# Scan: differences by products of 18 rows, and the diagonal with its inputs as stationary operand

## The chip, the cores and the metric

The kernel runs on one core of a Trainium2 chip. The metric is the device time in microseconds of one execution; the time of the kernel before is a median of three runs. Below, TensorE is the matrix engine (PE in the rows, PEld its weight loads), VectorE is DVE, ScalarE is ACT, GpSimd is POOL, and SyncE (SP, its queue SPq) issues the transfers.

## The reference

The program is one layer of a hybrid block over 16 meta tokens and 2048 frames of width 1024: an input projection, a stick-breaking attention, a Mamba-2 scan (SSD), an output projection. The change touches the scan alone, whose chunks the kernel makes 128 steps long:

```python
xdt = x * dt[..., None]
a_cum = jnp.cumsum(dt * a.reshape(G, R), axis=2)
seg = a_cum[:, :, :, None] - a_cum[:, :, None]
decay_ls = jnp.exp(jnp.where(causal, seg, -jnp.inf))
cb = jnp.einsum("bclgn,bcsgn->bclsg", cm, bm)
y_diag = jnp.einsum("bclsg,bclsgr,bcsgrp->bclgrp", cb, decay_ls, xdt)
decay_to_end = jnp.exp(a_cum[:, :, -1:] - a_cum)
states = jnp.einsum("bclgn,bclgr,bclgrp->bcgrpn", bm, decay_to_end, xdt)
chunk_decay = jnp.exp(a_cum[:, :, -1])
def step(h, inp):
    st, dec = inp
    return h * dec[..., None, None] + st, h
y_off = jnp.einsum("bclgn,bcgrpn,bclgr->bclgrp", cm, h_start, jnp.exp(a_cum))
y = y_diag + y_off + x * d_skip.astype(f32).reshape(G, R)[:, :, None]
```

There are 16 heads of 64 columns in two groups of 8 (G, R = 2, 8), and a state of 128 rows. `seg` is the difference of two running sums; only its exponential for later minus earlier steps is used.

## The kernel before, in words

The program runs four stages one behind the other: front (the input projection), the scan's setup (`scan_start`) and the scan (`scan_stage`), attention, output. A stage ends for all engines together, and each stage loads what the next one needs first where it can.

The scan has 16 chunks of 128 steps (`NT`), two groups of 8 heads each, so 32 units (s, g, i): s is the parity of the chunk, g the group, i the pair of chunks. The buffers of the inputs, `xc` (x, B and C of one chunk) and `zt` (its gate), are there twice, one for each s. `pipeline` writes out the order on each engine: at step n it calls a list of parts, each with how many units ahead of n it works. On TensorE the order in a step is front(n+1), turn(n-1), multiply(n). front makes, for g = 0, the transposes of B and C·B (`pbc`) and the running sums (`pc`), then for every unit the transposes of x (`px`) and the differences (`pseg`); turn transposes the sum of unit n-1 for its store (into `pyd`); multiply makes the product with the old state (`pyo`), the new state's part (`pst`) and the diagonal part (`pyd`). On GpSimd the order is spread_steps(n+2), skip(n+1), gate(n-1). All products are float32.

`before(s, g, i)` gives the unit ahead of one, so that a bank is not overwritten before its reader is done. SyncE stores and loads in one written order, and a wait in it holds back all that stands behind:

```python
store(s, 0, i)
if more:
    sp.wait_ge(off_done[s][1], i + 1 + START)
    sp.wait_ge(xd_ready[s][1], i + 1 + START)
    scan.load_xc(sp, s, i + 1)
store(s, 1, i)
if more:
    scan.load_zt(sp, s, i + 1)
```

So the load of the inputs of chunk c+1 is issued behind the store of group 0 of chunk c-1, which waits for `gate` of that unit on GpSimd; and front of the first unit of chunk c+1 waits on TensorE for the load (`xc_loaded`). Of the 16 loads of `xc` two are made by the setup and 14 by this loop.

Of the kernel before, what the change touches and what calls it, by code (L numbers as in the profile page):

```python
# [18 lines left out]
ALU = mybir.AluOpType  # L19
ACT = mybir.ActivationFunctionType  # L20
# [18 lines left out]
HPG = HEADS // GROUPS  # L39
CONV = 4  # L40
# [1149 lines left out]
class ScanEarly(Early):  # L1190


    def __init__(self, nc, ctx, scratch, d_cols):
# [6 lines left out]
        self.zt = [self.sbuf(f"s_zt{s}", [P, KB, P]) for s in range(2)]  # L1200
        self.d_loaded, self.filled, self.made = self.sem("d_loaded"), self.sem("s_filled"), self.sem("s_made")
# [32 lines left out]
def scan_start(nc, scratch, dt_tok, state, scan, attention):  # L1234

    with ExitStack() as ctx:
# [10 lines left out]
        ps = m.psum("s0_ps", [P, GROUPS, W])  # L1247
        loaded, made, ready = m.sem("s0_loaded"), m.sem("s0_made"), m.sem("s0_ready")
# [13 lines left out]
        def _(pool):  # L1262
            nc.gpsimd.memset(ident[:, :], 0.0).then_inc(made, 1)
# [6 lines left out]
            scan.constants(pool)  # L1270
# [3 lines left out]
        def _(pe):  # L1274
            pe.wait_ge(ready, START + 2)
# [13 lines left out]
        def _(act):  # L1289
            act.wait_ge(turned, START + 1)  # L1290
# [4 lines left out]
        def _(dve):  # L1295
            dve.wait_ge(turned, START + 1)
# [12 lines left out]
def scan_stage(nc, scratch, dt_tok, state, scan, attention):  # L1309
# [5 lines left out]
    with ExitStack() as ctx:  # L1315
# [6 lines left out]
        expo = [m.sbuf(f"s_expo{s}", [P, 3, HEADS]) for s in range(2)]  # L1322
        cbm = [m.sbuf(f"s_cbm{s}", [P, GROUPS, P]) for s in range(2)]
        ua = [m.sbuf(f"s_ua{g}", [P, HPG, P]) for g in range(GROUPS)]
# [5 lines left out]
        ysum = [m.sbuf(f"s_ysum{g}", [P, W]) for g in range(GROUPS)]  # L1330
# [5 lines left out]
        pc = m.psum("s_pc", [P, 3, HEADS])  # L1336
# [22 lines left out]

        def dt_of(i, s, which, g):  # L1360
# [3 lines left out]
            return dt_tok[:, bass.ds(i * 2 + (1 + s), 1), which, g * HPG:(g + 1) * HPG].rearrange("p o h -> p (o h)")  # L1364

# [21 lines left out]
        def _(sp):  # L1387
# [24 lines left out]
        def _(pool):  # L1412
# [22 lines left out]
            pipeline(pool, (2, spread_steps), (1, skip), (-1, gate))  # L1435

        @block.tensor
        def _(pe):
            pe.wait_ge(made, START + 4)

            def front(s, g, i):
                if g == 0:
# [9 lines left out]
                    pe.wait_ge(expo_ready[1 - s], i + s + START)  # L1452
                    for n, lhs in enumerate((upper, later, ones)):
                        rhs = (dt_tok[:, 1 + 2 * i + s, 1, :] if isinstance(i, int) else
                               dt_tok[:, bass.ds(i * 2 + (1 + s), 1), 1, :].rearrange("p o h -> p (o h)"))
# [846 lines left out]
```

## Time and profile before

| what | before |
|---|---|
| median of 3 runs | 2749.34 us (2748.38 to 2751.9) |
| profiled execution | 2747.44 us, of which 2745.6 us are the span of the trace |
| mean granted clock of TensorE | 0.973 |
| PE busy | 2606.7 us (95%) |
| PEld busy | 1834.4 us (67%) |
| DVE busy | 1770.6 us (64%) |
| ACT busy | 1311.5 us (48%) |
| POOL busy | 1586.4 us (58%) |
| the scan's first instructions | 1155.00 us |
| the attention's first instructions | 1394.77 us |

Shares are of the whole span. Positions in the trace are in us from its start, and the granted clock is a share of 2.4 GHz: 1.00 is that level, 0.50 is 1.2 GHz.

### The profile page before, as it was taken

The numbers are of one execution on the slowest core, as the hardware profiler recorded it, in microseconds if no ns is written. First come the engines' busy times: TensorE is split into PE (matmuls) and PEld (weight loads), VectorE is DVE, ScalarE is ACT, GpSimd is POOL, SyncE is SP. The second block draws the span as 40 slices with busy tenths as digits, with TensorE's granted clock in tenths as the row PEclk, the third lists the DMA queues.
The fourth block names the chain that finished last, engine by engine and source line by source line (L and its number), as shares of the span: only waits on it lengthen the run. The fifth ranks groups of instructions, "written<-read, shape, count | busy, mean of one in ns | idle before, by whom it ended". The sixth has DMA issues, their size and how long they took to land. (4 is left out here: it accounts for less than half of the span.)

```text
span 2745.6 us, 41086 instructions
## 1 busy us (share of the span) xinstructions
PE 2606.7 (95%) x14122; PEld 1834.4 (67%) x14122; DVE 1770.6 (64%) x2152; ACT 1311.5 (48%) x2072; POOL 1586.4 (58%) x1222
## 2 busy tenths in 40 slices
PE   5999999989999999799989999999999999599998
PEld 3788777767888888566645555555555555388887
DVE  5532565644214554299969888898888889555554
ACT  4433333434333333211158777787778777322221
POOL 5876666688777777478746565665666666000000
PEclk7999999999999999899979999999999999799999
DMA  2543323323333323244541212303122111333231
GB/s 104 154 157 111 124 86 132 116 89 129 128 123 138 123 99 132 70 115 131 148 135 55 71 49 61 93 24 93 55 62 78 40 40 58 123 119 107 76 113 40
DMA packets 202405, 267.95 MB, mean 98 GB/s; under 512 B 12833, under 2 KB 136033, under 8 KB 195569
## 3 DMA queue, kind: packets, MB, share of 16 engines
q1 hardware_dynamic: 202224, 265.64, 30.4%
q8 instruction: 102, 1.67, 0.3%
q14 instruction: 79, 0.64, 0.1%
HBM read 168.84 MB, written 96.76 MB: 97 GB/s over the span
## 5 line engine op out<-in xcount | busy, mean ns | idle before, releaser
L1969 POOL TENSOR_TENSOR a_w<-a_beta,a_rest 128x1024 f32<-128x1024 f32 (+2 forms) x320 | 560.3, 1751 | 354.0 <-DVE a_rest L1926 207.3
L763 POOL TENSOR_TENSOR f_l_lo<-f_wst,f_l_hi 128x512 fp32r<-128x512 f32 x312 | 405.0, 1301 | 269.1 <-ACT f_l_hi L631 268.8
L1926 DVE TENSOR_TENSOR_SCAN a_rest<-a_keep,a_rest,a_ones 128x513 f32<-128x513 f32 x384 | 470.0, 1262 | 10.8 <-ACT a_keep L1896 10.8
L1846 PE MATMUL a_turn<-a_ident,a_w 128*128 128x128 f32 (+1 forms) x2432 | 342.9, 279 | 7.3 <-DVE a_wt L1880 6.1
L1861 PE MATMUL a_o<-a_wt,a_v 128*64 128x512 f32 (+3 forms) x1408 | 339.4, 560 | 8.9 <-DVE a_out L1936 8.9
L499 PE MATMUL f_xz<-f_t_hi,f_l_hi 128*128 128x512 f32 x832 | 330.2, 397 | 6.9 <-issue 4.4
L499 PE MATMUL f_xz<-f_t_hi,f_l_lo 128*128 128x512 f32 x832 | 326.3, 392 | 0.0
L499 PE MATMUL f_xz<-f_t_lo,f_l_hi 128*128 128x512 f32 x832 | 326.0, 392 | 0.0
L1880 ACT COPY a_wt<-a_turn 128x512 f32<-128x512 f32 (+3 forms) x440 | 225.1, 528 | 207.0 <-PE a_turn L1846 205.5
L1846 PEld LDWEIGHTS a_turn<-a_ident,a_w 128*128 128x128 f32 (+1 forms) x2432 | 256.7, 140 | 91.5 <-issue 65.8
L1896 ACT ACTIVATE a_keep<-a_z 128x1024 f32<-128x1024 f32 (+4 forms) x352 | 300.1, 852 | 4.6 <-PE a_z L1829 4.5
L1896 ACT ACTIVATE a_beta<-a_z 128x1024 f32<-128x1024 f32 (+4 forms) x352 | 300.2, 853 | 0.0
L631 ACT ACTIVATE f_l_hi<-f_wst 128x512 fp32r<-128x512 f32 x312 | 195.9, 628 | 201.7 <-PE f_y L499 105.3
L499 PE MATMUL f_y<-f_t_hi,f_l_hi 128*128 128x512 f32 x624 | 248.6, 398 | 10.0 <-DVE f_work L1125 6.5
L499 PE MATMUL f_y<-f_t_lo,f_l_hi 128*128 128x512 f32 x624 | 244.7, 392 | 0.0
L499 PE MATMUL f_y<-f_t_hi,f_l_lo 128*128 128x512 f32 x624 | 244.3, 392 | 0.0
L1926 DVE TENSOR_TENSOR_SCAN a_rest<-a_keep,a_ones 128x144 f32<-128x144 f32 (+3 forms) x256 | 206.9, 837 | 44.5 <-ACT a_keep L1896 44.4
L1819 PEld LDWEIGHTS a_z<-a_k_high,a_q_high 64*128 64x128 f32 x704 | 66.6, 186 | 248.6 <-issue 219.2
L2143 PE MATMUL o_acc<-o_w_hi,o_g_hi 128*128 128x512 f32 x512 | 202.8, 396 | 20.8 <-DVE o_w_lo L2197 17.7
L1880 DVE COPY a_wt<-a_turn 128x512 f32<-128x512 f32 (+3 forms) x264 | 158.5, 600 | 71.9 <-PE a_turn L1846 71.2
L2143 PE MATMUL o_acc<-o_w_hi,o_g_lo 128*128 128x512 f32 x512 | 200.7, 392 | 0.0
L2143 PE MATMUL o_acc<-o_w_lo,o_g_hi 128*128 128x512 f32 x512 | 200.5, 392 | 0.0
(242 smaller groups left out, 4472.7 us busy)
## 6 DMA issues: line engine op xcount, KB each, us to landing
f_wst<-in_w_pairs SPq DMA_DIRECT2D x52, 1024.0 KB, 5.5
scratch_gate<-f_out SPq DMA_DIRECT2D x64, 256.0 KB, 2.2
o_g<-scratch_mixed SPq DMA_DIRECT2D x32, 512.0 KB, 5.5
s_xc<-scratch_xbc SPq DMA_DIRECT2D x16, 768.0 KB, 5.3
scratch_xbc<-f_out SPq DMA_DIRECT2D x36, 256.0 KB, 2.1
scratch_q_hi<-f_out SPq DMA_DIRECT2D x32, 256.0 KB, 3.5
scratch_q_lo<-f_out SPq DMA_DIRECT2D x32, 256.0 KB, 3.6
scratch_v<-f_out SPq DMA_DIRECT2D x32, 256.0 KB, 2.3
```

The costliest lines, as they stand in the source:

```text
L499: last = nc.tensor.matmul(BANKS[i][:, :], lhs[:, k, :], rhs[:, k, :], start=(i < 3 and k == 0 and lhs is hi and rhs is t_hi[i]), stop=(k = ...
L631: nc.scalar.activation(l_hi[m % RING][:, :, :], left_source(n, i), ACT.Copy).then_inc(left_hi, 1)
L763: return nc.gpsimd.tensor_tensor(out, a, b, op).then_inc(done, 1)
L1819: mm = nc.tensor.matmul(z[n % 2][:, h, 0:tn], q_part[ch % 2][rows, qb * P:(qb + 1) * P], k_part[slot][rows, t0:t0 + tn], start=(i == 0), s ...
L1846: mm = nc.tensor.transpose(turn[h][0:rows, qi * P:(qi + 1) * P], tile[:, h, x:x + rows], ident[:, :])
L1861: mm = nc.tensor.matmul(o[h * HEAD:(h + 1) * HEAD, first_q:W], v[pair % 2][0:rows, b, h * HEAD:(h + 1) * HEAD], wt[m % ATS][0:rows, h, fir ...
L1880: copy(wt[m % ATS][0:rows, h, first_q:W], turn[h][0:rows, first_q:W]).then_inc(done, 1)
L1896: nc.scalar.activation(tile[side(n) % KEEPS][:, :, lo:lo + tn], z[n % 2][:, :, 0:tn], ACT.Sigmoid, scale=scale).then_inc(done, 1)
L1926: mm = nc.vector.tensor_tensor_scan(rest[r % RS][:, h, tn - 1::-1], top, ones[:, 0:1].to_broadcast([P, tn]), start, ALU.mult, ALU.min)
L1969: nc.gpsimd.tensor_tensor(w[r % AS][:, :, 0:tn], beta[r % KEEPS][:, :, 0:tn], rest[r % RS][:, :, 1:tn + 1], ALU.mult).then_inc(w_ready, 1)
L2143: mm = nc.tensor.matmul(acc[n][q][:, :], lhs[s][:, k, :], rhs[:, k, n * W:(n + 1) * W], start=(k == q * KB and lhs is g_hi and rhs is w_hi ...
```

## The change

- The differences. Before, GpSimd spread the steps of 8 heads over a triangle (`ua`, 128x1024 values a unit), and TensorE multiplied it by a triangle of ones over 128 rows in float32. Now the setup makes the running sums of all chunks by step, splits each in a high and a low part (float32r), and writes them to memory (`scratch["cum"]`); each unit loads them back as two operands of 18 rows: `lag` (16 rows with the sums of 8 heads in two parts, two rows of ones) and `rise` (16 constant rows of -1 that select a head, two rows with the sums). The product of both is the difference, in float32r. ScalarE then makes two passes in place of one: Relu with scale -1, and Exp with scale -1.
- The running sums. The three small products and their exponential (`pc`, `expo`) leave the loop; the setup makes them for all chunks (`sums`).
- The diagonal. Before, the weights `mt` were the stationary operand and 64 columns of `xdt` moved, 8 products a unit. Now 64 columns of `xdt` are the stationary operand and 128 columns of `mt` move, 8 products, even heads into partitions 0 to 63 and odd ones into 64 to 127; the result is already transposed.
- The offset. `yo` is no longer added on VectorE (`ysum` is gone) and then transposed; it is multiplied by the identity in a float32 product that adds to `pyd`.
- Two operations move from VectorE to GpSimd: `xde` (to_end) and the decay of the state (fade), in front of skip and gate.
- SyncE issues 6 small loads more for each chunk, and the setup 4 small stores and 12 small loads.

The diff, cut:

```diff
+    def load_spans(self, sp, s, g, i):
+        steps = self.scratch["cum"][:, bass.ds(i * 2 + s, 1), g * HPG:(g + 1) * HPG, :]
+        sp.dma_start(self.rise[s][g][SPANS - 2:SPANS, :, :].bitcast(F32),
+                     steps.rearrange("q o h l -> q (o h) l")).then_inc(self.rise_loaded[s][g], 16)
+        for q in range(2):
+            sp.dma_start(self.lag[s][g][q * HPG:(q + 1) * HPG, :].bitcast(F32),
+                         steps[q, :, :, :].rearrange("o h l -> (o h) l")).then_inc(self.rise_loaded[s][g], 16)
...
+            scan.constants(pool)
+            nc.gpsimd.memset(own[:, :, :], 0.0).then_inc(own_step, 1)
+            for q in range(2):
+                pool.wait_ge(own_step, START + q + 1)
+                nc.gpsimd.affine_select(out=own[:, :, :], in_=own[:, :, :], compare_op=ALU.not_equal, fill=-1.0,
+                                        base=-q * HPG, pattern=[[-1, HPG], [0, P]], channel_multiplier=1).then_inc(own_step, 1)
...
+                    if more:
+                        for g in range(GROUPS):
+                            sp.wait_ge(seg_ready[s][g], i + 1 + START)
+                            scan.load_spans(sp, s, g, i + 1)
                     store(s, 0, i)
...
-            def spread_steps(s, g, i):
-
-                pool.wait_ge(seg_ready[1 - s][g], i + s + START)
-                nc.gpsimd.tensor_tensor(ua[g][:, :, :], upper[:, :].unsqueeze(1).to_broadcast([P, HPG, P]),
-                                        over_heads(dt_of(i, s, 1, g), P), ALU.mult).then_inc(ua_ready[s][g], 1)
+            def to_end(s, g, i):
+
+                hs = slice(g * HPG, (g + 1) * HPG)
+                pool.wait_ge(xdt_ready[s][g], i + 1 + START)
+                pool.wait_ge(st_done[1 - s][g], i + s + START)
+                nc.gpsimd.tensor_tensor(heads(xde[g]), heads(xdt[g]), over_heads(sums_of(i, s, 1, hs), HEAD),
+                                        ALU.mult).then_inc(xde_ready[s][g], 1)
+
+            def fade(s, g, i):
+
+                hs = slice(g * HPG, (g + 1) * HPG)
+                pool.wait_ge(off_done[s][g], i + 1 + START)
+                own = state[:, g, :].rearrange("p (h c) -> p h c", h=HPG)
+                nc.gpsimd.tensor_tensor(own, own, over_heads(sums_of(i, s, 2, hs), HEAD), ALU.mult).then_inc(decayed[s][g], 1)
...
-            pipeline(pool, (2, spread_steps), (1, skip), (-1, gate))
+            pipeline(pool, (1, to_end), (0, fade), (1, skip), (-1, gate))
...
-                    last = nc.tensor.matmul(pseg[:, hs, :], later[:, :], ua[g][:, hs, :], start=True, stop=True)
+                    last = nc.tensor.matmul(pseg[:, hs, :], scan.lag[s][g][:, :], scan.rise[s][g][:, hs, :], start=True, stop=True)
...
-                    last = nc.tensor.transpose(pyd[:, b * P:(b + 1) * P], ysum[g][:, b * P:(b + 1) * P], ident[:, :])
+                    last = nc.tensor.matmul(pyd[:, b * P:(b + 1) * P], yo[g][:, b * P:(b + 1) * P], ident[:, :],
+                                            start=False, stop=True, skip_group_check=True)
...
-                    last = nc.tensor.matmul(pyd[:, h * HEAD:(h + 1) * HEAD], mt[g][:, h, :],
-                                            xdt[g][:, h * HEAD:(h + 1) * HEAD], start=True, stop=True)
+                    rows, cols = slice(h % 2 * HEAD, (h % 2 + 1) * HEAD), slice(h // 2 * P, (h // 2 + 1) * P)
+                    last = nc.tensor.matmul(pyd[rows, cols], xdt[g][:, h * HEAD:(h + 1) * HEAD], mt[g][:, h, :],
+                                            start=(h < 2), stop=False, skip_group_check=True)
...
-                nc.scalar.activation(decay[g][:, :, :], pseg[:, :, :], ACT.Exp).then_inc(decay_ready[s][g], 1)
+                nc.scalar.activation(decay[g][:, :, :], pseg[:, :, :], ACT.Relu, scale=-1.0).then_inc(span_ready[s][g], 1)
+                act.wait_ge(span_ready[s][g], i + 1 + START)
+                nc.scalar.activation(decay[g][:, :, :], decay[g][:, :, :], ACT.Exp, scale=-1.0).then_inc(decay_ready[s][g], 1)
...
-                own = state[:, g, :].rearrange("p (h c) -> p h c", h=HPG)
-                nc.vector.tensor_tensor(own, own, over_heads(expo[s][:, 2, hs], HEAD), ALU.mult).then_inc(decayed[s][g], 1)
                 dve.wait_ge(decayed[s][g], i + 1 + START)
...
-            pipeline(dve, (1, inputs), (-1, add_skip), (0, states), (1, weights), (0, sum_y))
+            pipeline(dve, (1, inputs), (-1, add_skip), (0, states), (1, weights))
```

On TensorE, one unit with g = 1 in the loop, before (`pseg` the differences, the first `pyd` row the transposes of turn, the last one the diagonal):

```order
L1461 MATMUL s_px<-s_ident,s_xc 128x128 x4
L1467 MATMUL s_pseg<-s_ua,s_later 128x512 x2
L1473 MATMUL s_pyd<-s_ident,s_ysum 128x128 x4
L1480 MATMUL s_pyo<-state,s_xc 128x512
L1485 MATMUL s_pst<-s_xde,s_b 128x512
L1489 MATMUL s_pyd<-s_xdt,s_mt 128x64 x8
```

and now:

```order
L1540 MATMUL s_px<-s_ident,s_xc 128x128 x4
L1546 MATMUL s_pseg<-s_rise,s_lag 128x512 x2
L1552 MATMUL s_pyd<-s_ident,s_yo 128x128 x4
L1560 MATMUL s_pyo<-state,s_xc 128x512
L1565 MATMUL s_pst<-s_xde,s_b 128x512
L1570 MATMUL s_pyd<-s_mt,s_xdt 64x128 x8
```

The order is the same; the turn is a product of `yo` and stands ahead of `pyo` as before, and the diagonal has 128 moving columns in place of 64.

On GpSimd, two units ahead of the loop, before, with buffer numbers, which are the group's (`ua` is spread_steps, `xd` skip, `gated` gate):

```order
L1419 TENSOR_TENSOR s_ua1<-s_upper,dt_tok 128x1024
L1425 TENSOR_TENSOR s_xd0<-s_xc1,s_d_col 128x512
L1432 TENSOR_TENSOR s_gated0<-s_yt0,s_zt0 128x512
L1419 TENSOR_TENSOR s_ua0<-s_upper,dt_tok 128x1024
L1425 TENSOR_TENSOR s_xd1<-s_xc1,s_d_col 128x512
L1432 TENSOR_TENSOR s_gated1<-s_yt1,s_zt0 128x512
```

and now (`xde` is to_end, `state` fade):

```order
L1497 TENSOR_TENSOR s_xde0<-s_xdt0,s_sums 128x512
L1505 TENSOR_TENSOR state<-state,s_sums 128x512
L1510 TENSOR_TENSOR s_xd0<-s_xc1,s_d_col 128x512
L1517 TENSOR_TENSOR s_gated0<-s_yt0,s_zt0 128x512
L1497 TENSOR_TENSOR s_xde1<-s_xdt1,s_sums 128x512
L1505 TENSOR_TENSOR state<-state,s_sums 128x512
L1510 TENSOR_TENSOR s_xd1<-s_xc1,s_d_col 128x512
L1517 TENSOR_TENSOR s_gated1<-s_yt1,s_zt0 128x512
```

The gate of a unit has moved behind fade, an operation that waits for `pyo` of the unit after it.


## Rows read from the trace of the kernel before

**Rows 1.** Stretch of the scan: length, PE, PEld, DVE, ACT, POOL busy, PEclk, DMA share, GB/s

```profile
1210.00:1240.00 30.00, 29.72 (x171) 20.88 (x170) 29.05 (x37) 5.89 (x10) 24.40 (x14) 1.00 0.47 124
```

**Rows 2.** Timeline of the scan; start us, us, engine, line, operation, tiles

```profile
1251.95 1.58 DVE L1540 TENSOR_TENSOR s_mt<-s_decay,s_cbm 128x1024 f32<-128x1024 f32 x1
...
1252.02 0.44 PE L1447 MATMUL s_pbc<-s_ident,s_xc 128*128 128x128 f32 x2 [0.25 <-DMA s_xc<-scratch_xbc]
...
1252.40 2.88 POOL L1419 TENSOR_TENSOR s_ua<-s_upper,dt_tok 128x1024 f32<-128x1024 f32 x1
...
1252.74 0.29 PE L1456 MATMUL s_pc<-dt_tok,s_upper 128*128 x2
...
1253.33 0.63 PE L1461 MATMUL s_px<-s_ident,s_xc 128*128 128x128 f32 x4
...
1253.80 1.88 PE L1467 MATMUL s_pseg<-s_ua,s_later 128*128 128x512 f32 x4
...
1255.52 0.60 PE L1473 MATMUL s_pyd<-s_ident,s_ysum 128*128 128x128 f32 x4
...
1255.95 1.02 PE L1480 MATMUL s_pyo<-state,s_xc 128*128 128x512 f32 x2
...
1257.67 1.90 PE L1489 MATMUL s_pyd<-s_xdt,s_mt 128*128 128x64 f32 x16
...
1259.40 0.61 PE L1461 MATMUL s_px<-s_ident,s_xc 128*128 128x128 f32 x4
...
1259.89 0.39 SPq L1390 DMA_DIRECT2D scratch_mixed<-s_gated  x1
...
1260.54 0.38 SPq L1205 DMA_DIRECT2D s_xc<-scratch_xbc  x1
...
1265.80 0.44 PE L1447 MATMUL s_pbc<-s_ident,s_xc 128*128 128x128 f32 x2
```

**Rows 3.** DMA issues of the page; times, KB each, median us to landing

```profile
s_xc<-scratch_xbc SPq DMA_DIRECT2D x16, 768.0 KB, 5.3
```

**Rows 4.** Timeline, TensorE alone, attention

```profile
1906.18 1.08 PE L1861 MATMUL a_o<-a_wt,a_v 128*64 128x512 f32 x4
```

**Rows 5.** Timeline of the last products ahead of the scan

```profile
1120.35 0.39 PE L499 MATMUL f_y<-f_t_hi,f_l_hi 128*128 128x512 f32 x1
...
1120.58 0.39 PE L499 MATMUL f_y<-f_t_lo,f_l_hi 128*128 128x512 f32 x1
```

**Rows 6.** Instructions that touch four tiles of the scan; ns min/median/max

```profile
L1419 POOL TENSOR_TENSOR s_ua<-s_upper,dt_tok x32: 1894/2874/2882, 1155.0 to 1363.6; 128x1024 f32<-128x1024 f32 x32
...
L1432 POOL TENSOR_TENSOR s_gated<-s_yt,s_zt x32: 1261/1718/1727, 1174.8 to 1388.2; 128x512 f32<-128x512 f32 x32
...
L1425 POOL TENSOR_TENSOR s_xd<-s_xc,s_d_col x32: 1038/1039/2019, 1158.7 to 1374.4; 128x512 f32<-128x512 f32 x32
...
L1540 DVE TENSOR_TENSOR s_mt<-s_decay,s_cbm x32: 1220/1573/1966, 1163.2 to 1376.6; 128x1024 f32<-128x1024 f32 x32
```

**Rows 7.** Costliest groups, ScalarE; xcount, busy us, mean ns, idle before

```profile
L1507 ACT ACTIVATE s_decay<-s_pseg 128x1024 f32<-128x1024 f32 x32 | 32.8, 1025 | 112.0 <-PE s_pseg L1467 112.0
```

**Rows 8.** Timeline, end of the scan

```profile
1378.87 1.11 PE L1473 MATMUL s_pyd<-s_ident,s_ysum 128*128 128x128 f32 x4 [2.29 <-DVE s_ysum L1560]
```

**Rows 9.** Timeline, TensorE alone, a gap in the attention

```profile
2129.10 1.97 PE L1861 MATMUL a_o<-a_wt,a_v 128*64 128x512 f32 x4 [1.11 <-DVE a_out L1936]
```

**Rows 10.** Timeline of the setup in front of the scan

```profile
1139.69 0.28 POOL L1226 TENSOR_SCALAR_AFFINE_SELECT s_upper<-s_upper 128x128 f32<-128x128 f32 x1
...
1140.45 4.50 SPq L1209 DMA_DIRECT2D s_zt<-scratch_gate  x2
...
1140.93 1.86 PE L1278 MATMUL s_px<-s_ident,s_xc 128*16 128x128 f32 x8 [8.18 <-DMA s_xc<-scratch_xbc]
...
1149.81 1.23 DVE L1306 COPY state<-s_ps 128x1024 f32<-128x1024 f32 x1 [3.93 <-PE s_ps L1285]
1155.00 3.75 POOL L1419 TENSOR_TENSOR s_ua<-s_upper,dt_tok 128x1024 f32<-128x1024 f32 x2 [13.04 <-POOLq L64]
```

More of the change, by code:

```diff
@@ L39 @@
 HPG = HEADS // GROUPS
+SPANS = 2 * HPG + 2
 CONV = 4
@@ L1200, in __init__ @@
         self.zt = [self.sbuf(f"s_zt{s}", [P, KB, P]) for s in range(2)]
+        self.sums = self.sbuf("s_sums", [P, 3, NT, HEADS])
+        self.lag = [[self.sbuf(f"s_lag{s}{g}", [SPANS, P], F32R) for g in range(GROUPS)] for s in range(2)]
+        self.rise = [[self.sbuf(f"s_rise{s}{g}", [SPANS, HPG, P], F32R) for g in range(GROUPS)] for s in range(2)]
+        self.rise_loaded = [self.sems(f"s_rise_loaded{s}", GROUPS) for s in range(2)]
         self.d_loaded, self.filled, self.made = self.sem("d_loaded"), self.sem("s_filled"), self.sem("s_made")
@@ L1269, in _ @@
                                     pattern=[[-1, META]], channel_multiplier=1).then_inc(ready, 1)
-            scan.constants(pool)
             attention.constants(pool)
@@ L1274, in _ @@
         def _(pe):
+            pe.wait_ge(scan.made, 4)
+            pe.wait_ge(steps_ready, START + 1)
+            for b in range(2):
+                last = nc.tensor.matmul(ps[:, b, 0:P],
+                                        steps[:, b * (NT // 2):(b + 1) * (NT // 2), :].rearrange("p t h -> p (t h)"),
+                                        scan.upper[:, :], start=True, stop=True)
+            last.then_inc(cum_done, 1)
+            for q, lhs in enumerate((scan.upper, scan.later, scan.ones)):
+                last = nc.tensor.matmul(psums[:, q, :], lhs[:, :], steps[:, :, :].rearrange("p t h -> p (t h)"),
+                                        start=True, stop=True)
+            last.then_inc(sums_done, 1)
             pe.wait_ge(ready, START + 2)
@@ L1289, in _ @@
         def _(act):
+            act.wait_ge(cum_done, START + 1)
+            for b in range(2):
+                nc.scalar.activation(by_step[0][b][:, :], ps[:, b, 0:P], ACT.Copy).then_inc(cum_high, 1)
+            act.wait_ge(sums_done, START + 1)
+            nc.scalar.activation(scan.sums[:, :, :, :].rearrange("p q t h -> p q (t h)"), psums[:, 0:3, :],
+                                 ACT.Exp).then_inc(sums_ready, 1)
+            act.wait_ge(own_step, START + 3)
+            for s in range(2):
+                for g in range(GROUPS):
+                    nc.scalar.activation(scan.rise[s][g][0:2 * HPG, :, :], own[:, :, :], ACT.Copy).then_inc(own_kept, 1)
             act.wait_ge(turned, START + 1)
@@ L1295, in _ @@
         def _(dve):
+            nc.vector.tensor_copy(steps[:, :, :], dt_tok[:, 1:NT + 1, 1, :]).then_inc(steps_ready, 1)
+            for s in range(2):
+                for g in range(GROUPS):
+                    nc.vector.memset(scan.lag[s][g][:, :].bitcast(F32), 1.0).then_inc(lag_ones, 1)
+            for b in range(2):
+                dve.wait_ge(cum_high, START + b + 1)
+                nc.vector.tensor_tensor(by_step[1][b][:, :], ps[:, b, 0:P], by_step[0][b][:, :].bitcast(F32),
+                                        ALU.subtract).then_inc(cum_low, 1)
             dve.wait_ge(turned, START + 1)
@@ L1329, in scan_stage @@
         yo = [m.sbuf(f"s_yo{g}", [P, W]) for g in range(GROUPS)]
-        ysum = [m.sbuf(f"s_ysum{g}", [P, W]) for g in range(GROUPS)]
         xd = [m.sbuf(f"s_xd{g}", [P, GB, P]) for g in range(GROUPS)]
@@ L1364, in dt_of, with sums_of @@
             return dt_tok[:, bass.ds(i * 2 + (1 + s), 1), which, g * HPG:(g + 1) * HPG].rearrange("p o h -> p (o h)")
+        def sums_of(i, s, which, hs):
+            if isinstance(i, int):
+                return scan.sums[:, which, 2 * i + s, hs]
+            return scan.sums[:, which, bass.ds(i * 2 + s, 1), hs].rearrange("p o h -> p (o h)")
         def pipeline(eng, *stages):
@@ L1394, in step @@
                 for s in range(2):
+                    if more:
+                        for g in range(GROUPS):
+                            sp.wait_ge(seg_ready[s][g], i + 1 + START)
+                            scan.load_spans(sp, s, g, i + 1)
                     store(s, 0, i)
@@ L1451, in front @@
                     last.then_inc(bc_ready[s], 1)
[L1452 to L1455, printed above, removed]
-                        last = nc.tensor.matmul(pc[:, n, :], lhs[:, :], rhs, start=True, stop=True)
-                    last.then_inc(sums_ready[s], 1)
                 ps, pg, count = before(s, g, i)
```

60 lines of the change are left out of this document (32 added, 28 removed).

## The prediction, made before the changed kernel ran

> **What bounds the kernel now.** The change lies in one stage, so I read that stage, from its totals to its single instructions.
>
> First the busy time in a stretch of the scan [rows 1]. In 30 us TensorE is busy for 29.72 and VectorE for 29.05, GpSimd for 24.40, ScalarE for 5.89. Two engines are full, so relief for one alone would do little; the change relieves both. The clock is 1.00.
>
> Then the timeline of one pair of units, one chunk [rows 2]. TensorE starts the chunk at 1252.02 and the next at 1265.80: 13.78 us. I read its terms from start to start, since the durations overlap: B, C and C·B 0.72 (1252.02 to 1252.74), running sums 0.59, x 0.47, differences 1.72, turn 0.43, old and new state together 1.72 (0.86 each), diagonal 1.73 (to 1259.40); the second unit takes the other 6.40.
>
> The same view shows a third bound, which the totals hide. The first row says what TensorE waited for last: 0.25 us for the load of `xc`. The load for the chunk that begins at 1265.80 is issued at 1260.54, and such a load lands after 5.3 us [rows 3]: 1265.8. So a cycle runs through the loop, of front, turn, gate on GpSimd, store, load, landing, and front again: 8.52 us from front's start to the load's issue (1252.02 to 1260.54) and 5.3 of landing, 13.8. It is as long as TensorE's own work. Whatever is saved on TensorE, a chunk can't be shorter than this cycle. So the question is what the change does to the cycle.
>
> **The change, part by part.**
>
> TensorE's own work. The running sums leave: -0.59 a chunk. The differences become two float32r products of 512 columns; such products start 0.23 apart [rows 5], so 0.46 in place of 1.72. No row has one with 18 rows; I take 0.46 for it, at worst the 1.72 that it was, and at best nothing less, since the columns are the same. The turn becomes a float32 product that streams 4x128 columns, as many as the 512 of the product with the old state, which costs 0.86: +0.43. The diagonal streams 8x128 columns. One by one that is twice 0.86, 1.72, no change. But the attention has two float32 products of 512 columns whose outputs lie in different halves of the partitions, and both together take 1.08 to their end [rows 4], where one takes 1.02 [rows 2]: they run side by side. So the diagonal, four such pairs of 128 columns, is about 1.0; I take 1.1. Sum for a unit: -1.26 +0.43 -0.63 = -1.46, and for a chunk 2x1.46 + 0.59 = 3.5: TensorE has 10.3 us of work a chunk (up to 11.5 with the diagonal at 1.72).
> The Trainium skill (TensorEngine Tiling, Theoretical Speedup) gives up to a factor of 2 where one dimension is 64 or less; with it the diagonal would be 0.87 and the chunk 0.5 shorter in TensorE's work, and the attention's pair comes near it, 1.08 for two where one takes 1.02.
>
> VectorE. `xde`, `ysum` and the decay of the state leave. By `mt`, 1.58 for 1024 columns [rows 2], these three of 512 are about 0.8 each, 2.4 of its 6.7 us a unit (29.05 of 30 of 6.9). It has some 4.3 left and waits for others.
>
> ScalarE. A second pass like its first, 1.03 [rows 7]: it has little work [rows 1], and the weights are needed only after turn, `pyo` and `pst`, about a unit later. Nothing, while that cover stands; without it 1.0 a unit.
>
> GpSimd. `ua` (2.87 a unit) goes; to_end and fade come, each of the form of skip (128x512 with a spread operand, 1.04 [rows 6]): -0.8 a unit in busy time. What counts is the place. gate(n-1) stands behind fade(n), which waits for `pyo` of unit n; before, it stood behind skip, and neither of the two waits for `pyo`.
>
> SyncE. 6 small loads a chunk, in front of a store. At 0.65 from issue to issue (1259.89 to 1260.54 [rows 2]) they are 3.9 us between two stores more than 5 us apart: hidden, and 0 on the cycle. If they took 1.0 each, 6 us, the store would be late by about 1.
>
> **The cycle now**, from front's start, uncontended:
> - front: 0.72 + 0.47 + 0.46 = 1.65
> - turn 0.86, then `pyo` 0.86 and 0.15 until it has drained (its row lasts 1.02): 1.87
> - on GpSimd fade 1.04, skip 1.04, gate 1.26 (its shortest [rows 6]): 3.34
> - the load is issued 0.65 behind the store, and I give 0.4 to the three handovers between engines: 1.05
> - together 7.9, and with 5.3 of landing 13.2.
>
> So even unhindered the cycle is 0.6 shorter than before, where TensorE's work is 3.5 shorter. The rest becomes a wait for `xc`.
>
> Two things come on top. **The weights' multiplication holds GpSimd up.** `ua` takes 1.89 at its shortest and 2.87 in the loop, and gate 1.26 and 1.72 [rows 6]. In the timeline `mt` (two operands in SBUF) lasts to 1253.53 and `ua` begins at 1252.40 [rows 2]: 1.13 us side by side, and 0.98 lost, 0.87 for each us. Now `mt` starts when fade and the addition to the state (0.6) are over, that is in the last part of skip, and covers gate: 1.57x0.87 = 1.4 us on the cycle, if it overlaps in full; none, if it falls before. I take 1.3: 14.5.
> The Trainium skill (GPSIMD Engine Reference, Specifications) says that GpSimd shares its SBUF interfaces with VectorE, with contention from instructions with two SBUF inputs; the rows of `mt` agree, and it speaks for the loss, since the four operations on GpSimd now meet the one of that kind that VectorE keeps.
>
> **The clock.** TensorE would stand still for 14.5 - 10.3 = 4.2 us in each chunk. At the end of the scan it stood still for 2.29 us, and the turn behind it took 1.11 where it takes 0.60 [rows 2, 8]; a pair of the attention took 1.97 in place of 1.08 behind 1.11 us of standing still [rows 4, 9]. So after such waits the clock is at 1.2 GHz, and what comes right behind the wait is front, turn and `pyo`, all of it on the cycle, 3.4 us at 2.4 GHz. If the clock stays down for all of it the cycle is 14.5 + 3.4 = 17.9; if it comes back in the middle, 16.2. I take 17.1.
>
> **The sum.** 14 loads of `xc` are in the loop. 14 x (17.1 - 13.8) = +46. The last two chunks wait for no load: 2 x (10.3 - 13.8) = -7, of which I keep -5, since the chain of the state stays. The setup: TensorE's transposes begin at 1140.93 [rows 10], and now wait for a constant that stands behind a clearing and two selections over 1024 columns. A selection over 128 columns takes 0.28; if it grows in proportion, 2 each, 5 us of GpSimd, from about 1140 to 1145, so 4 us late. In the same time ScalarE has four copies of 1024 columns, about 1 us each by [rows 7]. At the end SyncE has 12 small loads behind the rest of its list; the two `zt` loads alone held it for 4.50 [rows 10], and the list starts some 4 us late behind the stores of the sums. The stage behind starts 4 us after the last work (1151.04 to 1155.00). I take +7, bounds +3 and +11. Sum: +46 -5 +7 = +48. The profiled execution took 2747.44, so 2795; the median lies 1.9 above it, of which I add half: 2796.
>
> **The rivals.**
> - The clock holds (15%). For it: the waits of 0.25 in the loop left it at 1.00. Against it: the two waits of [rows 8, 9]. Then 14 x (14.5 - 13.8) = +10, -5 +7: 2760; with a smaller overlap of `mt` 2750 to 2762.
> - Faster (12%). `mt` falls beside to_end and not beside gate, and the clock holds: 14 x (13.2 - 13.8) = -8, with -7 in the last chunks and +5 for the setup: 2738. What decides is the cycle's part ahead of the load: it must be under 8.5 us; it does this only with the clock up. If moreover the load lands sooner than 5.3, 1 us less gives 14 less again, and with TensorE's work as the bound, 10.3, 14 x -3.5 -2 = -51: 2698.
> - All of the loop at half clock (8%). TensorE's work is then 20 us a chunk and the bound: 14 x 6.5 + 7 and more for the last chunks: about 2850. Against it: work without a gap brings the clock back.
> - The diagonals don't run side by side, 1.72. For it: the loads of the stationary operands. TensorE only fills a part of its wait: within 5 of the forecast. Here it changes no chance.
> - No difference (5%): the clock holds, `mt` overlaps gate in part, a cycle of 13.6 to 13.9 and the setup paid by the end.
>
> The forecast itself, a longer cycle and a lowered clock, has 60%, and its own range from a cycle of 15.6 (+25 -5 +5) to one of 18.3 with +11: 2772 to 2818. Together with the case of the clock that holds, and what lies between, 2750 to 2818 holds about 8 in 10; faster and half clock lie outside. A measurement of this kernel can tell about 0.2%, 5.5 us, from no change. Faster 0.13, the same 0.07, slower 0.80.
>
> **What would show it.** In the timeline of the loop: TensorE's first row of each chunk waits for `xc`, 2 to 5 us; the load is issued over 9 us behind front's start; gate takes about 2 to 2.6; chunks are 16 to 18.3 apart; the granted clock of the stretch is between 0.6 and 0.85, and front's rows take twice their time. The 8 diagonal products take 1.0 to 1.2 at full clock. VectorE falls to under two thirds busy. The scan starts near 1162. The prediction is wrong if the wait for `xc` is short: then the gate comes earlier than I work out, or the load lands sooner; or if the clock stays at 1.00 through waits of 3 us.

## The result, and the profile after

The changed kernel takes 2777.82 us (2776.37 to 2785.35, 4 runs), the kernel before in the same runs 2748.86: a ratio of 1.0109, 95% interval 1.0089 to 1.0129, 29 us slower.

The page's first part, busy time by engine, and two stretches of the loop, with the columns of [rows 1]:

```profile
PE 2590.6 (93%) x14100; PEld 1815.0 (65%) x14100; DVE 1694.7 (61%) x2063; ACT 1346.9 (49%) x2095; POOL 1576.5 (57%) x1257
```

```profile
1215.00:1245.00 30.00, 24.42 (x142) 14.99 (x140) 17.32 (x22) 9.09 (x10) 19.47 (x16) 0.89 0.45 120
1245.00:1275.00 30.00, 22.46 (x118) 14.30 (x114) 13.13 (x18) 7.01 (x8) 16.74 (x14) 0.77 0.46 120
```

TensorE, full before, is now busy for 24.4 and 22.5 of 30 us, VectorE for 17.3 and 13.1 and no longer 29.05, and the clock was granted at 0.89 and 0.77. There is less work in a stretch, and the chunks take longer. The grouped waits between 1200 and 1380 us say what it waited for (total us, times, longest):

```profile
PE s_pbc L1532 <- DMA s_xc<-scratch_xbc: 34.4, 12, 3.9
```

Twelve chunks wait for `xc`, 2.9 us each in the mean. The timeline (columns as in [rows 2]) shows a chunk, from 1265.81 to 1282.75, the end of the one ahead and the start of the one behind:

```profile
1256.79 1.44 DVE L1612 TENSOR_TENSOR s_mt<-s_decay,s_cbm 128x1024 f32<-128x1024 f32 x1
1257.11 2.26 POOL L1517 TENSOR_TENSOR s_gated<-s_yt,s_zt 128x512 f32<-128x512 f32 x1
...
1260.18 0.40 SPq L1210 DMA_DIRECT2D s_xc<-scratch_xbc  x1
...
1265.81 0.69 PE L1532 MATMUL s_pbc<-s_ident,s_xc 128*128 128x128 f32 x2 [3.92 <-DMA s_xc<-scratch_xbc]
...
1267.14 1.06 PE L1540 MATMUL s_px<-s_ident,s_xc 128*128 128x128 f32 x4
...
1268.13 1.22 PE L1546 MATMUL s_pseg<-s_rise,s_lag 18*128 18x512 f32 x2
...
1269.28 2.08 PE L1552 MATMUL s_pyd<-s_ident,s_yo 128*128 128x128 f32 x8
...
1271.15 1.91 PE L1560 MATMUL s_pyo<-state,s_xc 128*128 128x512 f32 x2
...
1274.70 1.19 PE L1570 MATMUL s_pyd<-s_mt,s_xdt 128*64 128x128 f32 x16
...
1275.25 1.27 POOL L1517 TENSOR_TENSOR s_gated<-s_yt,s_zt 128x512 f32<-128x512 f32 x1
1275.48 2.12 DVE L1612 TENSOR_TENSOR s_mt<-s_decay,s_cbm 128x1024 f32<-128x1024 f32 x1
...
1277.40 0.39 SPq L1210 DMA_DIRECT2D s_xc<-scratch_xbc  x1
...
1279.87 1.09 PE L1570 MATMUL s_pyd<-s_mt,s_xdt 128*64 128x128 f32 x16
...
1282.75 0.44 PE L1532 MATMUL s_pbc<-s_ident,s_xc 128*128 128x128 f32 x2 [1.78 <-DMA s_xc<-scratch_xbc]
...
1283.47 0.60 PE L1540 MATMUL s_px<-s_ident,s_xc 128*128 128x128 f32 x4
...
1284.66 1.16 PE L1552 MATMUL s_pyd<-s_ident,s_yo 128*128 128x128 f32 x8
```

The load issued at 1260.18 has landed at 1265.81, after 5.6; gate, which its store waits for, took 2.26 beside `mt`. TensorE waited 3.92 us, and from here its rows take about twice as long, x 1.06 and turn 2.08 where the next chunk has 0.60 and 1.16, the old state 1.91 for 1.02 [rows 2]: the clock is at 1.2 GHz. The next load is issued at 1277.40, 11.6 us behind front's start, where it was 8.5 before, and 5.35 later the next front begins. From the first row of `pbc` of chunk 2 to that of chunk 15, counted from 0, the mean spacing is 15.96 us; before it was 13.88. That mean is of two kinds: of the 14 spacings from chunk 1 to 15 five are 14.5 to 14.7, at full clock, and nine 15.9 to 17.5, with a part at half clock.

The timeline of the setup, with the last of the 12 small loads in the row of 1156.94 and the scan's first product in the last row:

```profile
1141.16 2.31 POOL L1300 TENSOR_SCALAR_AFFINE_SELECT s_own<-s_own 16x1024 f32<-16x1024 f32 x2
...
1144.37 1.44 PE L1327 MATMUL s_px<-s_ident,s_xc 128*16 128x128 f32 x8 [0.42 <-POOL s_later L1307]
...
1145.89 5.98 SPq L1214 DMA_DIRECT2D s_zt<-scratch_gate  x2
...
1153.89 1.23 DVE L1373 COPY state<-s_ps 128x1024 f32<-128x1024 f32 x1 [3.93 <-PE s_ps L1334]
...
1156.94 0.61 SPq L1222 DMA_DIRECT2D s_lag<-scratch_cum  x2
...
1161.79 0.66 PE L1532 MATMUL s_pbc<-s_ident,s_xc 128*128 128x128 f32 x2 [7.94 <-PEq L65]
```

TensorE starts the scan at 1161.79; before, it did at 1155.18, just behind GpSimd [rows 10]: +6.6. Both selections over 1024 columns together take 2.31. SyncE's list ends last, at 1157.55, where VectorE's last work ends at 1155.12; the scan starts 4.2 behind the list. From the scan's first product to the attention's first (line 1819 before, 1884 now) it is 261.5 us, before 239.8: +21.7. The 14 chunks that wait for a load of the loop begin within 222.0 us, before 194.4 (1168.58 to 1362.98), so they have 27.6 more; the first spacing has 2.3 less and the end of the last chunk 3.6 less.

### The profile page after: what moved, and what is told of

The parts are those of the page before. It is cut to its first block and busy times, and to the rows that moved or that the text cites. A ratio compares the mean times of both kernels' runs of the same rounds, so it can differ in the third digit from the quotient of the medians.

```text
span 2774.7 us, 41294 instructions
## 1 busy us (share of the span) xinstructions
PE 2590.6 (93%) x14100; PEld 1815.0 (65%) x14100; DVE 1694.7 (61%) x2063; ACT 1346.9 (49%) x2095; POOL 1576.5 (57%) x1257
```

## The experiments

Eleven kernels ran, in three groups on the same chip each, so that those of one group share their runs of before (2748.5, 2747.83 and 2749.32 us). The spacing is the mean between chunks 2 and 15, read from the timeline as above; "issue" is how many us behind front's start the load of `xc` is issued, the loop's first load left out. Spacing and issue are of the profiled execution alone.

| kernel | us | ratio to before (95%) | spacing | issue |
|---|---|---|---|---|
| before | 2748.86 | | 13.88 | 8.5 |
| changed | 2777.82 | 1.0109 (1.0089 to 1.0129) | 15.96 | 9.2 to 12.3 |
| load first | 2721.80 | 0.9901 (0.9884 to 0.9917) | 11.75 | 5.5 to 7.1 |
| before, load first | 2744.91 | 0.9988 (0.9979 to 0.9998) | 13.67 | 5.1 |
| gate first | 2735.29 | 0.9950 (0.9934 to 0.9967) | 12.78 | 7.1 to 8.6 |
| filler products | 2759.22 | 1.0043 (1.0028 to 1.0057) | 14.43 | 9.2 |
| both on VectorE | 2745.13 | 0.9988 (0.9978 to 0.9998) | 13.81 | 7.5 to 9.5 |
| both on VectorE, load first | 2729.07 | 0.9932 (0.9916 to 0.9949) | 12.24 | 5.8 to 6.1 |
| to_end on VectorE, load first | 2718.23 | 0.9889 (0.9873 to 0.9906) | 11.52 | 5.5 to 7.1 |
| and setup in another order | 2716.11 | 0.9885 (0.9868 to 0.9901) | 11.48 | 5.3 to 7.0 |
| and load ahead of the small loads | 2709.96 | 0.9861 (0.9844 to 0.9877) | 10.98 | 4.1 to 4.5 |
| changed, load ahead of all | 2715.39 | 0.9872 (0.9855 to 0.9890) | 11.02 | 4.1 to 4.6 |
| heads apart | 2721.90 | 0.9904 (0.9888 to 0.9921) | 11.79 | 4.1 |

**Load first.**

```diff
-                    store(s, 0, i)
                     if more:
                         sp.wait_ge(off_done[s][1], i + 1 + START)
                         sp.wait_ge(xd_ready[s][1], i + 1 + START)
                         scan.load_xc(sp, s, i + 1)
+                    store(s, 0, i)
```

> The changed kernel, with one edit on SyncE: the load of xc is issued ahead of the store of group 0, so that it waits for the product with the old state and for skip, no longer for gate. My theory (the cycle front, turn, fade, skip, gate, store, load, landing bounds the loop): the load is issued some 4 us behind front's start, lands at 9.3, TensorE's own work of about 10.3 us a chunk becomes the bound, the clock stays up; chunks 10.3 to 11.2 apart, time 2778 - 14 x 5 = 2700 to 2712. Rival A (GpSimd's four operations or the chain of the state bound the loop, the load is only seen last): the chunks stay within 0.5 us of 15.9, time 2770 to 2780. Rival B (the products are too thin for the full clock, with 18 rows and half the columns): no wait is left, but the granted clock stays well under 1 and the chunks are 14 us or more apart, 2750 or more.

The load has moved ahead of a store, and the change, which made the kernel 29 us slower, makes it 27 us faster. So the load's cycle was the bound at a spacing of 16, not GpSimd and not the state, and the clock is back. One of its windows, columns as above:

```profile
1215.00:1245.00 30.00, 27.36 (x187) 18.01 (x187) 20.61 (x27) 11.47 (x14) 26.63 (x21) 0.97 0.62 166
```

The size is missed: a spacing of 11.75 and not 10.3 to 11.2. The wait for `xc` is not gone, and GpSimd is busy for 26.6 of 30; which of the two it is, the runs below tell.

**The same edit in the kernel before.**

> The kernel before, with the same edit on SyncE. My theory: there TensorE's own work (13.78 less the wait of about 0.25) and the load's cycle were equally long; only the wait goes, 0.1 to 0.25 us a chunk: 2745 to 2749, and no more, since VectorE and TensorE are full. Rival A: no change at all. If the load alone had been the bound of before, and not the engines, it would be 2735 or less.

As expected (2745 to 2749): the spacing is 13.67 for 13.88, the wait goes, 0.2 a chunk, and the bound that stood beside it, the engines' work, is left. The same move is worth 4 us in the kernel before and 56 in the changed one.

**Gate first.**

```diff
-            pipeline(pool, (1, to_end), (0, fade), (1, skip), (-1, gate))
+            pipeline(pool, (1, to_end), (-1, gate), (0, fade), (1, skip))
```

> The changed kernel, with one edit on GpSimd: gate stands ahead of fade and skip. My theory: the cycle loses fade and skip (2.1 us) and gate meets the weights' multiplication no longer; the load is issued 5.5 to 6 us behind front's start, chunks 10.8 to 11.8 apart, the clock near 1: 2702 to 2720. Rival A (GpSimd's total or the state's chain): fade now comes 1.3 us later, so the loop stays at 15.9 or grows: 2775 to 2795. Rival B (thin products): clock still below 0.9, 2750 or more.

Well faster than the changed kernel, so gate's place did lengthen the cycle, but 12.78 and not 11.8: the rival had a part in it. The grouped waits between 1200 and 1340 us:

```profile
DVE state L1625 <- POOL state L1505: 49.1, 22, 2.4
...
PE s_pyd L1570 <- DVE s_yt L1631: 10.7, 13, 1.0
PEld s_pbc L1532 <- DMA s_xc<-scratch_xbc: 8.4, 10, 1.2
```

VectorE now waits 2.2 us a unit for fade, `yt` stands behind that wait in VectorE's order, and the diagonal waits for `yt`. Gate and fade are both urgent, and one engine does them one behind the other.

**Filler products.** 12 products into a bank that nobody reads; nothing is left out.

```diff
+                if g == 1:
+                    for _ in range(12):
+                        nc.tensor.matmul(pfill[:, 0:P], ident[:, :], upper[:, :], start=True, stop=True)
```

> The changed kernel, with 12 float32 products of 128 columns (0.21 us each at full clock, 2.6 together) into a bank that nobody reads, behind the diagonal of each second unit, where TensorE waits for xc. It adds work and takes no wait away. My theory: TensorE no longer stands still, the clock is near 1.00 in the loop, front, turn and the old state's product run at full rate in every chunk, and the cycle is the one with gate held up, 14.3 to 14.9: time 2778 - 14 x 1.3 = 2755 to 2765. Rival C (the clock costs nothing here, because its loss lies in TensorE's wait): no change, 2775 to 2781, though the clock rises. Rival B (thin products): the clock stays under 0.95.

Two stretches of its windows:

```profile
1245.00:1275.00 30.00, 28.42 (x205) 20.27 (x205) 17.64 (x24) 10.25 (x12) 22.02 (x17) 1.00 0.49 129
1275.00:1305.00 30.00, 28.47 (x202) 19.58 (x200) 18.10 (x24) 9.74 (x11) 22.00 (x18) 1.00 0.51 133
```

More work, and 18.6 us less time (2777.82 to 2759.22). A chunk of its timeline and the start of the next:

```profile
1257.15 0.44 PE L1533 MATMUL s_pbc<-s_ident,s_xc 128*128 128x128 f32 x2 [0.83 <-DMA s_xc<-scratch_xbc]
...
1262.89 2.94 PE L1576 MATMUL s_pfill<-s_upper,s_ident 128*128 128x128 f32 x24
...
1266.40 0.40 SPq L1210 DMA_DIRECT2D s_xc<-scratch_xbc  x1
...
1271.07 2.25 POOL L1518 TENSOR_TENSOR s_gated<-s_yt,s_zt 128x512 f32<-128x512 f32 x1
...
1271.52 0.44 PE L1533 MATMUL s_pbc<-s_ident,s_xc 128*128 128x128 f32 x2 [0.75 <-DMA s_xc<-scratch_xbc]
```

The clock is at 1.00. The load is issued 9.25 behind front's start (1257.15 to 1266.40) and has landed 5.12 later, together 14.37 in this chunk and 14.43 in the mean. Gate takes 2.25. So the clock cost 1.5 us a chunk in the mean (15.96 less 14.43), and the cycle alone, at full clock, is 0.55 longer than before.

**Both on VectorE.** `to_end` goes to the end of `inputs`, fade behind `yo` in `states`, as before.

```diff
-            pipeline(pool, (1, to_end), (0, fade), (1, skip), (-1, gate))
+            pipeline(pool, (1, skip), (-1, gate))
...
+                nc.vector.tensor_tensor(heads(xde[g]), heads(xdt[g]), over_heads(sums_of(i, s, 1, hs), HEAD),
+                                        ALU.mult).then_inc(xde_ready[s][g], 1)
...
+                nc.vector.tensor_tensor(own, own, over_heads(sums_of(i, s, 2, hs), HEAD), ALU.mult).then_inc(decayed[s][g], 1)
```

> The changed kernel with one part of the change undone: to_end and fade are back on VectorE, at the places that they had before; GpSimd has skip and gate alone. SyncE's order is that of the changed kernel. My theory (gate's place behind fade lengthened the load's cycle): gate comes as early as before and on TensorE's shorter terms, the load is issued 6.7 to 7.5 us behind front's start, the chunks are 12.0 to 12.9 apart: 2722 to 2736, with a short wait for xc. Rival D (the longer cycle came from the other parts, the offset's product, Relu's pass or the small loads of SyncE): the chunks stay at 14 us or more, 2750 or more.

It lies between the two: 2745 us, where the rival had 2750 and more and I had 2722 to 2736. The spacing of 13.81 is that of the slowest of its ten runs (2751.69 us); at the median it is some 0.5 less, an estimate from 6.6 us over 14 chunks. The load comes later than I worked out, for three reasons that the timeline shows (turn, xde, yt, skip, gate, load):

```profile
1255.61 1.16 PE L1552 MATMUL s_pyd<-s_ident,s_yo 128*128 128x128 f32 x8
...
1257.06 0.69 DVE L1611 TENSOR_TENSOR s_xde<-s_xdt,s_sums 128x512 f32<-128x512 f32 x1 [0.15 <-DVE s_xdt L1606]
...
1257.67 0.68 DVE L1638 TENSOR_TENSOR s_yt<-s_xd,s_pyd 128x512 f32<-128x512 f32 x1
...
1258.43 1.04 POOL L1510 TENSOR_TENSOR s_xd<-s_xc,s_d_col 128x512 f32<-128x512 f32 x1 [3.54 <-DVE s_yt L1638]
...
1259.43 1.73 POOL L1517 TENSOR_TENSOR s_gated<-s_yt,s_zt 128x512 f32<-128x512 f32 x1
...
1262.04 0.39 SPq L1210 DMA_DIRECT2D s_xc<-scratch_xbc  x1
```

Turn has drained at 1256.77, but `yt` waits for `xde` ahead of it on VectorE and begins at 1257.67; skip waits for `yt`, not gate alone; and gate takes 1.73 beside fade, which VectorE runs from 1258.87 to 1260.02. A gap of TensorE stays, and with it a clock of 0.84 to 0.91. That the move to GpSimd alone made the change slow is thus true in part only: with the two on VectorE the change gives 3 us (0.9988), and not the 40 that the fastest kernel below gives.

**The same with the load first.** The edit is the sum of this one and that of the first experiment.

> to_end and fade on VectorE as in the run before, and the load of xc ahead of the store of group 0. No wait for xc is left. My theory: VectorE is then the bound, at the 13.4 us a chunk that it had less ysum, 12.0 to 12.4: it is busy for 95% or more, chunks 12.0 to 12.5 apart, 2722 to 2732, so no faster than with both operations on GpSimd (11.75). Rival E (TensorE's own work of 10.3 is the bound wherever the two stand): 10.3 to 11.0, 2700 to 2712.

A stretch of its windows:

```profile
1245.00:1275.00 30.00, 26.96 (x183) 17.16 (x182) 29.09 (x37) 11.22 (x13) 12.83 (x11) 1.00 0.58 152
```

As expected: VectorE (third number) is the bound at 29.09 of 30, and TensorE has room. This is what the move to GpSimd was good for: the same order of loads with both on GpSimd is at 11.75.

**to_end on VectorE, fade on GpSimd, load first.**

```diff
-            pipeline(pool, (1, to_end), (0, fade), (1, skip), (-1, gate))
+            pipeline(pool, (0, fade), (1, skip), (-1, gate))
```

> to_end on VectorE, fade on GpSimd, and the load of xc ahead of the store of group 0. In the run with the load first GpSimd was busy for 27 of 30 us, the chunks were 11.75 apart. My theory: GpSimd was that bound; now it has some 8.7 us a chunk, VectorE 10, and TensorE's 10.3 bounds: chunks 10.4 to 11.1 apart, 2703 to 2713. Rival F (the landing of xc, with more bytes in flight, or the waits within a unit bound it): 11.5 or more, 2718 or more.

The rival was right: 11.52, hardly less than 11.75, though GpSimd is busy for 22 of 30 us now and no longer 27. GpSimd was not the bound of the run with the load first. SyncE's rows ahead of a load say what was:

```profile
1256.41 0.40 SPq L1214 DMA_DIRECT2D s_zt<-scratch_gate  x1
...
1257.01 0.37 SPq L1219 DMA_DIRECT2D s_rise<-scratch_cum  x1
...
1257.47 0.76 SPq L1222 DMA_DIRECT2D s_lag<-scratch_cum  x2
...
1258.41 0.24 SPq L1219 DMA_DIRECT2D s_rise<-scratch_cum  x1
...
1258.74 0.74 SPq L1222 DMA_DIRECT2D s_lag<-scratch_cum  x2
...
1259.71 0.40 SPq L1210 DMA_DIRECT2D s_xc<-scratch_xbc  x1
```

Behind `zt` stand six small loads (two rows each have two of them), 2.7 us from 1257.01 to the load at 1259.71. I had put the small loads at nothing, since they fit between the stores; with the load in front of the store they stand in front of the load.

**And the setup in another order.** In this kernel `own` is made behind `later`, the four copies stand behind the copy of B, and the first loads of `xc` ahead of the stores of the sums:

```diff
+            for s in range(2):
+                scan.load_xc(sp, s, 0)
             sp.wait_ge(cum_high, START + 2)
...
-            scan.loads(sp)
+            for s in range(2):
+                scan.load_zt(sp, s, 0)
+            sp.dma_start(scan.d_col[:, :], scan.d_cols).then_inc(scan.d_loaded, 16)
...
+            act.wait_ge(turned, START + 1)
+            nc.scalar.activation(decay[:, :], pd[:, :], ACT.Exp).then_inc(decay_ready, 1)
+            nc.scalar.activation(b_tok[:, :, :], pb[:, :, :], ACT.Copy).then_inc(b_ready, 1)
             act.wait_ge(own_step, START + 3)
```

> The run before, and the setup in another order: the constant of -1 behind those that TensorE's transposes wait for, its four copies on ScalarE behind the exponential and the copy of B, and the first two loads of xc ahead of the stores of the sums. My theory: the scan's first product starts 2.5 to 4 us earlier than in the changed kernel (1161.8), because SyncE's list ends earlier: 2 to 4 us less than the run before. Rival G (the end of the setup is set by the chain of the first state alone, 1.5 us): 1 to 1.5 us less.

The scan's first product is at 1159.18 and not 1162.08, and the kernel 2.1 us faster than the one without this edit, with runs that overlap (2715.41 to 2718.24 and 2716.59 to 2719.86). The start scatters: with the setup of the changed kernel it lies at 1159.83 to 1162.39 in eight traces, with this one at 1158.48 to 1159.67 in three. So some 2 us are gained, and since the three moves were made together, which of them gave it is not told apart.

**Load ahead of the small loads too**, first in that kernel, then in the changed one, where it is the only edit.

```diff
                     if more:
+                        sp.wait_ge(off_done[s][1], i + 1 + START)
+                        sp.wait_ge(xd_ready[s][1], i + 1 + START)
+                        scan.load_xc(sp, s, i + 1)
+                    if more:
                         for g in range(GROUPS):
                             sp.wait_ge(seg_ready[s][g], i + 1 + START)
                             scan.load_spans(sp, s, g, i + 1)
                     store(s, 0, i)
-                    if more:
-                        sp.wait_ge(off_done[s][1], i + 1 + START)
-                        sp.wait_ge(xd_ready[s][1], i + 1 + START)
-                        scan.load_xc(sp, s, i + 1)
```

> The run with to_end on VectorE and the setup in another order, and on SyncE the load of xc ahead of the six small loads too. In those runs the load was still issued 5.5 to 7 us behind front's start and TensorE waited for it 0.5 us or so a chunk; the timeline shows it right behind the small loads, which take 2.5 us behind zt. My theory (SyncE's written order holds the load back): it is issued some 4 us behind front's start, no wait is left, and TensorE's own work of 10.3 to 10.9 us bounds: 2716 - 14 x 0.7 = 2702 to 2710. Rival F (another wait within the units bounds at 11.5): within 3 us of 2716.

> The changed kernel with SyncE's order of the run before alone: the load of xc ahead of the store and of the small loads; to_end and fade stay on GpSimd, the setup is that of the changed kernel. My theory: no wait for xc is left; GpSimd's four operations, 1.04 three times and gate at 2.25 beside the weights' multiplication, 5.4 a unit, are the bound: chunks 10.8 to 11.4 apart, 2710 to 2720, GpSimd busy for 28 us of 30. Rival F: the chunks stay at 11.75 as with the load only ahead of the store, 2722.

In both the waits for `xc` are nearly gone (1.5 and 1.9 us in the whole loop, where the changed kernel has 41.5), and both are at 11.0. Chunks that nothing holds up are 10.82 apart: that is TensorE's own sum. The timeline of the first gives its terms at full clock (the diagonal, then the next front up to the load):

```profile
1246.24 1.09 PE L1574 MATMUL s_pyd<-s_mt,s_xdt 128*64 128x128 f32 x16
...
1247.33 0.44 PE L1536 MATMUL s_pbc<-s_ident,s_xc 128*128 128x128 f32 x2
...
1248.59 0.73 PE L1550 MATMUL s_pseg<-s_rise,s_lag 18*128 18x512 f32 x2
...
1249.24 1.16 PE L1556 MATMUL s_pyd<-s_ident,s_yo 128*128 128x128 f32 x8
...
1250.24 1.02 PE L1564 MATMUL s_pyo<-state,s_xc 128*128 128x512 f32 x2
...
1251.43 0.46 SPq L1210 DMA_DIRECT2D s_xc<-scratch_xbc  x1
```

In the second one GpSimd (its busy time stands ahead of the clock) is busy for 29 of 30 us, and still the spacing is that of the first, where it has 22 to 24: not GpSimd, which I expected, but TensorE is the bound of both.

```profile
1245.00:1275.00 30.00, 29.79 (x203) 19.26 (x202) 23.21 (x31) 12.90 (x15) 29.07 (x23) 1.00 0.59 160
```

So with SyncE's order alone the change is 1.3% faster than before (0.9872), and 2.2% faster than as it was made (2715.39 to 2777.82).

**Heads apart.** In the kernel with the load ahead of the small loads and the other setup, the diagonal's products with even heads first.

```diff
-                for h in range(HPG):
+                for h in (0, 2, 4, 6, 1, 3, 5, 7):
```

> The first kernel of this call with the diagonal's products in another order: heads 0, 2, 4, 6 and then 1, 3, 5, 7, so that neighbours write the same half of the partitions. Same products, same columns. My theory (neighbours in different halves run side by side): the eight products take 1.7 to 1.9 us in place of 1.0, TensorE's work grows by 1.4 to 1.7 us a chunk, chunks 11.8 to 12.4 apart, 20 to 27 us slower than that kernel. Rival H (the gain of the diagonal lies in the loads of the stationary operand, 64 columns in place of 128, and not in the halves): no difference, within 3 us.

TensorE's timeline of it:

```profile
1256.90 1.58 PE L1574 MATMUL s_pyd<-s_mt,s_xdt 128*64 128x128 f32 x16
1258.42 0.66 PE L1544 MATMUL s_px<-s_ident,s_xc 128*128 128x128 f32 x4
```

The eight products take 1.52 (1256.90 to 1258.42) where in turns they took 1.09 and 1.02. So products in different halves do run side by side. The size is under what I expected, 0.5 a unit and 12 us in all: in the single records of the trace the odd heads start at 1257.40, where the even ones go on to start until 1257.72, so that a part still runs side by side.

## Why the prediction was right, and where it was off

**What bounds it.** Right: a load's cycle as long as the engines' work, hidden in the totals. In the kernel before with the load first the spacing is 13.67, the engines' own; 13.88 was the cycle's. The change is slower, as forecast, but by 29 us and not 47: 2777.8 lies in the lower part of the range, because the clock's term was too large (below).

**TensorE's terms.** Right to 5%: 10.82 a chunk where nothing holds it up, for my 10.3. From start to start in the rows from 1246.24 to 1250.24 the differences take 0.65 for my 0.46, the turn 1.00 for 0.86, the diagonal 1.09 for 1.1. The surplus, 0.14 and 0.19, probably comes with the step from one kind of product to another, which I left out: the second record of turn starts 0.21 behind its first, the others 0.11 apart. No run isolates it. The products into different halves do run side by side: 1.09 for the eight in turns, 1.52 with the even heads first.
The Trainium skill (TensorEngine Tiling, Theoretical Speedup) gives up to a factor of 2 where one dimension is 64 or less; the trace agrees, with 1.09 for the 1.72 that I worked out one by one.

**The cycle.** Right in its mechanism: 14.43 with the clock up, against 14.5. That the size fits so well is in part luck, since errors cancel: gate takes 2.25 beside `mt`, 1.0 more than alone, for the 1.3 that I took, and the landing 5.12 to 5.2 for 5.3; from front's start to fade's it is 4.1 (1257.15 to 1261.26 with the filler), for 3.5 and a handover.

**The clock: the term that was too large.** I added 2.6 us to each of 14 chunks, 17.1 for 14.5. The filler run sizes it: 15.96 less 14.43 is 1.5. In the sum my +46 measured +27.6, and these 18.4 us are as large as the whole miss (2796 less 2777.8 is 18.2). About 16 of them are the clock; the rest is that the kernel before stands at 13.88 and not at 13.8, and the cycle at 14.43. Two things stand against what I assumed.

First, the clock is low in nine of the 14 chunks and not in all, and in some of the nine for a few products only; in the stretches it is 0.77 to 0.94, not 0.6 to 0.85. After the wait of 1.78 us at 1282.75 the first product took 0.44, full rate, where after 3.92 us at 1265.81 it took 0.69 and all behind it twice their time. The two kinds bring each other about. Behind a chunk at full clock, or slow for a few products only, TensorE waits 3.4 to 3.9 us, and the next chunk was slowed each time (at the latest from its differences on). A chunk that is slow up to the new state's part keeps TensorE busy for 14 to 15 us in place of 10.9, so the wait behind it is 1.4 to 1.8 us, and in four of five such cases the chunk that followed ran at full clock.

Second, the two surcharges are not to be added: in the five chunks that were slow so long, `mt` came late, gate began first (1275.25), and took 1.27 instead of 2.26.

**The rest of the sum.** Setup +6.6 for +7, though the share of GpSimd in it was wrong, 1.15 us for a selection over 1024 columns and not 2; SyncE's list set the end: in the traces of five kernels (changed, filler products, the two with the other setup, heads apart) the scan starts 4.2 to 4.3 us behind the list's last load, wherever that lies (1154.24 to 1157.55). In other runs with this setup the scan starts up to 2.0 us earlier, so the near hit is in part chance. The last chunk gave 3.6 and the first spacing 2.3, together 5.9 for the 5 that I took for two last chunks.

**The small loads.** Costed at nothing on the cycle; right in the changed kernel, since they are not between store and load, and wrong as soon as the load was moved: 0.5 us a chunk (11.48 to 10.98) and, with both operations on GpSimd, 0.7 (11.75 to 11.02).

**The rivals.** Faster needed the part ahead of the load to be under 8.5 us; it was 9.2 at full clock. The clock that holds did not come by itself; held by the filler it gives 2759, for the 2760 that I worked out.

What stays open: which waits lower the clock. In the changed kernel all nine waits of 3.4 to 3.9 us had rows at half rate behind them, and of the five of 1.4 to 1.8 us one had (that of 1.73 at 1361.50, from turn on). With both on VectorE one of 1.86 us had (1267.37), and in the kernel before those of 2.29 and 1.11 [rows 8, 9]. So the length alone does not tell, and no run here varied it alone.

## What to carry to other kernels

When the busiest engine gets less work, look first for the loop that runs through a load: from the wait on the data to the issue of the next load, all engines in it, and the landing. Its length is a second bound, and if it ties with the first, no saving shows. Operations that are moved to an idle engine for room can lengthen it by their place alone; and a written order of transfers, in which a load stands behind a store that it doesn't need, is the cheapest place to cut.

## What was not expected of the hardware

- Filler work made the kernel 18.6 us faster: 12 products a chunk kept the granted clock at 1.00, where it had been 0.77 to 0.94.
- Of gate on GpSimd and `mt` on VectorE the one that starts second pays most. In the rows of the changed kernel `mt` starts at 1256.79 and gate 0.32 later: `mt` 1.44, gate 2.26. At 1275.25 gate starts first and `mt` 0.23 later: gate 1.27, `mt` 2.12. Gate's 1.0 is lost over 1.12 us side by side, and `mt`'s 0.90, against 1.22 at its shortest [rows 6], over 1.04. It is so in all 30 units of the changed kernel that have both: 25 with `mt` first (gate 2.24 to 2.26) and 5 with gate first (gate 1.26 to 1.27, `mt` 2.02 to 2.21).
- A product of 18 rows is no cheaper than one of 128: two of 512 columns in float32r took 0.65 (1248.59 to 1249.24), where two of 128 rows, in a row of their kind, started 0.23 apart [rows 5]. Whether the rest is the step to another kind of product or the 18 rows, no run shows.
